# First layer of a two-block transformer kernel: value sums, merge and gate laid out by features, merging weights turned and repeated by DMA

## The reference, cut to what matters

```python
qkv = proj[..., :n_qkv].reshape(B, S, 3, N_DIL_GROUPS * DIL_HEADS, HEAD_DIM)
gate = proj[..., n_qkv:]
for g, (window, dil) in enumerate(DIL_GROUPS):       # (128,1), (512,4), (2048,16)
    o, lse = dilated_window_attention(q[:, :, sl], k[:, :, sl], v[:, :, sl], window, dil)
    outs.append(o); lses.append(lse)
alpha = jax.nn.softmax(jnp.stack(lses, axis=0), axis=0)
o = jnp.sum(alpha[..., None] * jnp.stack(outs, axis=0), axis=0)
y = o.reshape(B, S, DIL_WIDTH) * jax.nn.silu(gate)
return y @ w_out
```

## Time and profile before

| | |
|---|---|
| median of 3 runs | 2764.05 us (2762.17 to 2765.48) |
| profiled execution | 2763.36 us, span 2761.8 us |
| PE busy | 2699.4 us, 98% |
| PE weight loads | 2159.5 us, 78% |
| DVE, ACT, POOL busy | 1223.8, 1048.8, 1137.9 us |
| granted TensorE clock | 0.995 of full speed |
| chain that ended last | PE 93%, DVE 3%, ACT 2%, issue 1% |

### The profile page before, as it was taken

The page is one execution under the profiler, slowest core; times in us unless marked ns, Lnnn a source line. Parts: engine busy times, 40 slices in busy tenths (PEclk is TensorE's granted clock), DMA queues, the critical chain, the costliest instruction groups (busy, mean ns, idle before and its releaser), DMA issues.

```text
span 2761.8 us, 36052 instructions
## 1 busy us (share of the span) xinstructions
PE 2699.4 (98%) x13721; PEld 2159.5 (78%) x13721; DVE 1223.8 (44%) x2467; ACT 1048.8 (38%) x2005; POOL 1137.9 (41%) x894
## 2 busy tenths in 40 slices
PE   8999999999999999999999999999999999999998
PEld 6887878888778877776788888887777678888887
DVE  4434343443555356444236424265644423642425
ACT  3333434353345344452333424234445233342422
POOL 4434343434432443333364444444333336444442
PEclk9999999999999999999999999999999999999999
DMA  5434343432421332223252333324222325233331
GB/s 188 135 86 136 96 126 96 123 121 72 128 85 54 97 108 84 70 88 119 98 176 79 114 100 92 94 79 131 84 70 88 119 99 172 81 115 99 92 95 58
DMA packets 214912, 286.39 MB, mean 104 GB/s; under 512 B 16846, under 2 KB 154546, under 8 KB 213972
## 3 DMA queue, kind: packets, MB, share of 16 engines
q1 hardware_dynamic: 214740, 284.08, 33.6%
HBM read 248.31 MB, written 18.94 MB: 97 GB/s over the span
## 4 chain that ended last, share of the span: by engine, by line
PE 93%; DVE 3%; ACT 2%; issue 1%; POOL 0%; DMA 0%; DVEq 0%; ACTq 0%; POOLq 0%
PE banks L1652 37%; PE banks L1649 28%; PE banks L1645 13%; PE banks L1782 2%; PE banks L1670 2%; PE banks L1764 1%; PE banks L1868 1%; PE banks L1685 1%; PE banks L1709 1%; PE banks L1803 1%; PE banks L1891 1%; PE banks L1940 1%; PE banks L1854 1%; PE banks L1749 1%; PE banks L1825 1%
## 5 line engine op out<-in xcount | busy, mean ns | idle before, releaser
L2949 POOL TENSOR_TENSOR WS<-WR,WS 128x512 fp32r<-128x512 f32 (+2 forms) x676 | 854.2, 1295 | 1098.0 <-ACT WS L2003 1098.0
L1652 PE MATMUL banks<-WS,UT 128*128 128x512 f32 (+1 forms) x3696 | 800.3, 366 | 5.4 <-DVE UT L2360 5.4
L1652 PEld LDWEIGHTS banks<-WS,UT 128*128 128x128 f32 x3696 | 607.5, 190 | 135.7 <-issue 37.1
L1649 PE MATMUL banks<-UT,WS 128*128 128x512 f32 (+1 forms) x2832 | 661.3, 392 | 0.7 <-ACT AR L2190 0.7
L1649 PEld LDWEIGHTS banks<-UT,WS 128*128 128x128 f32 (+1 forms) x2832 | 526.7, 187 | 127.0 <-issue 17.0
L2003 ACT ACTIVATE WS<-WR 128x1024 fp32r<-128x1024 f32 (+1 forms) x344 | 333.0, 1018 | 223.0 <-PE banks L1652 153.6
L1645 PE MATMUL banks<-UT,WS 128*128 128x512 f32 x1536 | 374.1, 397 | 0.0
L1645 PEld LDWEIGHTS banks<-UT,WS 128*128 128x128 f32 x1536 | 283.4, 189 | 64.9 <-issue 6.2
L1652 PE MATMUL banks<-WS,AT 128*128 128x512 f32 x1296 | 308.2, 396 | 0.0
L2947 POOL TENSOR_TENSOR WS<-WR,WS 128x512 fp32r<-128x512 f32 x128 | 181.0, 1445 | 261.6 <-ACT WS L1999 261.6
L1652 PEld LDWEIGHTS banks<-WS,AT 128*128 128x128 f32 x1296 | 242.8, 188 | 58.2 <-ACT WS L2003 0.7
(11 more groups left out here) (225 smaller groups left out, 2679.2 us busy)
## 6 DMA issues: line engine op xcount, KB each, us to landing
WR<-in_w_in SPq DMA_DIRECT2D x112, 512.0 KB, 3.6
WR<-in_w_up SPq DMA_DIRECT2D x88, 512.0 KB, 3.5
WR<-in_dil_w_in SPq DMA_DIRECT2D x64, 512.0 KB, 3.9
WR<-in_w_down SPq DMA_DIRECT2D x40, 512.0 KB, 3.7
WR<-in_diff_w_in SPq DMA_DIRECT2D x32, 512.0 KB, 3.7
WR<-in_dil_w_in SPq DMA_DIRECT2D x32, 256.0 KB, 3.2
AR<-AF SPq DMA_DIRECT2D x128, 64.0 KB, 2.4
AR<-AF SPq DMA_DIRECT2D x64, 128.0 KB, 2.4
```

The lines of the kernel that those rows point to most:

```text
L1649: mm = pe.matmul(B[bank][0:c, :], w[part][:, kk, g * P:g * P + c], act[:, other, kk, :], start=start, stop=stop)
L1652: mm = pe.matmul(B[bank][:, off:off + n], act[:, other, before_k + kk, g * P:g * P + P], w[part][:, kk, :], start=start, stop=stop)
L2949: ge.tensor_tensor(slot(i, 1)[:, s], raw(i)[:, s], slot(i, 0)[:, s].bitcast(F32), ALU.subtract).then_inc(lo_p.sem, 1)
```

## The change

In `out1` the 64 columns of values are stationary and the turned weights move; head hh writes partitions 64·hh to 64·hh+63, and the order of the loops is key block outside, head inside. The sums so come out by features, far ones into `XT` (features x far order), near ones into `N0` (features x natural order), and only maxima and denominators (4 floats a token) go through `near`.

`merge1` is split. `share1` works out the shares on DVE; `rows1` turns the 128 x 16 shares into 16 rows by a PE transpose and an ACT eviction; `send1` stores the rows in DRAM (8 KB); `fetch1` loads them again, each row repeated over the 64 partitions of its head, by two DMAs of 256 KB; `merge1` then multiplies and adds by features. `send1`, `fetch1` and `merge1` are put into the list 2, 4 and 8 ticks after `rows1`.

The gate tiles become feature-major (`gates_by_features`), with `gate1` and `times1`, and the chunks with their 32 transposes are replaced by `parts1`, which makes high and low part from `XT` on ACT and DVE. R_G1 goes from 1.38 to 1.7.

```diff
-R0, R1, R2, R3, R_L1, R_L2, R_G1, R_G2 = 0.994, 1.0, 1.3, 0.54, 0.8, 1.2, 1.38, 1.35
+R0, R1, R2, R3, R_L1, R_L2, R_G1, R_G2 = 0.994, 1.0, 1.3, 0.54, 0.8, 1.2, 1.7, 1.35
+    def gates_by_features(self, ready, late):
+        for j in range(4):
+            while j < 3 and not ready(j):
+                self.tick()
+                yield 1
+
+            def deal(i, t, j=j):
+                self.step("gate1", i, t)
+                if j == 3:
+                    late.append((i, t, j))
+                else:
+                    self.step("times1", i, t, j)
+                    if j < 2:
+                        self.soon(4, lambda: self.step("parts1", 2 * j + t))
+            yield from self.feature_major(f"l1g{j}", deal)
...
                     self.step("weigh1", p)
                     yield
-                    self.step("merge1", p)
-                    merged.add(p)
+                    self.step("share1", p)
+                    yield
+                    self.step("rows1", p)
+
+                    def merge():
+                        self.step("merge1", p)
+                        merged.add(p)
+                    self.soon(2, lambda: self.step("send1", p))
+                    self.soon(4, lambda: self.step("fetch1", p))
+                    self.soon(8, merge)
                     yield
...
-        self.beside(self.gates("l1g", lambda j: 2 * j + 1 in merged, late), att, R_G1)
+        self.beside(self.gates_by_features(lambda j: 2 * j + 1 in merged, late), att, R_G1)
         self.lower(self.splits)
         self.drain(att)
+        self.flush()
...
-                       self.opening([("chunk", "l1g", c) for c in range(4, 8)]))
+                       self.opening([("parts1", c) for c in range(4, 8)]))
...
-                    for hh in range(2):
-                        r = 64 * hh
-                        for j in range(w // P):
+                    for j in range(w // P):
+                        for hh in range(2):
+                            r = 64 * hh
...
-                            mm = pe.matmul(B[ob][:, r:r + 64], fat(7168 + 512 * e + 256 * hh + j * P, P), vj,
+                            mm = pe.matmul(B[ob][r:r + 64, 0:P], vj, fat(7168 + 512 * e + 256 * hh + j * P, P),
                                            start=(j == 0), stop=(j == w // P - 1))
...
+                elif kind == "rows1":
+                    p, = a
+                    k = bank6["rows", p]
+                    pe.wait_ge(shared.sem, shared.at[p])
+                    pe.wait_ge(*before["rows", p])
+                    pe.transpose(B[k][0:16, 0:P], SM[:, QT + 16:QT + 32], IDN).then_inc(rows_turned.sem, 1)
...
+                elif kind == "merge1":
+                    p, = a
+                    by_rest = "p (l r) -> p r l"
+                    y, x = N0[p % 2].rearrange(by_rest, r=4), XT[:, p].rearrange("p (r l) -> p r l", r=4)
+                    s0, s1 = (shares[:, g].rearrange("p (r l) -> p r l", r=4) for g in range(2))
+                    ve.wait_ge(sums_out.sem, sums_out.at["1", l1_last(p, 1)])
+                    ve.wait_ge(rows_in, 32 * (p + 1))
+                    tt(y, y, s0, ALU.mult)
+                    tt(x, x, s1, ALU.mult).then_inc(dve_step, 1)
                     ve.wait_ge(dve_step, V.of())
+                    tt(x, x, y, ALU.add).then_inc(merged.sem, 1)
...
+                elif kind == "parts1":
+                    c, = a
+                    if c == 0:
+                        for name in "qk":
+                            se.wait_ge(*there(index[f"l1{name}23"]))
+                    if c == 4:
+                        se.wait_ge(merged.sem, merged.at[7])
+                    if c == 6:
+                        se.wait_ge(timed.sem, timed.at[index["l1g3"], 1])
+                    se.wait_ge(timed.sem, timed.at[index[f"l1g{c // 2}"], c % 2])
...
+                elif kind == "send1":
+                    p, = a
+                    sy.wait_ge(rows_out.sem, rows_out.at[p])
+                    if p > 0:
+                        sy.wait_ge(rows_sent, 16 * p)
+                    sy.dma_start(share_rows[p], turned_shares[0:16, :]).then_inc(rows_sent, 16)
+
+                elif kind == "fetch1":
+                    p, = a
+                    sy.wait_ge(rows_sent, 16 * (p + 1))
+                    if p > 0:
+                        sy.wait_ge(merged.sem, merged.at[p - 1])
+                    rows_of = share_rows[p].rearrange("(g r h) l -> h g r l", g=2, h=2)
+                    for h in range(2):
+                        sy.dma_start(shares[64 * h:64 * h + 64].rearrange("p g (r l) -> p g r l", r=4),
+                                     rows_of[h].unsqueeze(0).to_broadcast([64, 2, 4, P])).then_inc(rows_in, 16)
```

More of the change, by code:

```diff
@@ L991, in build @@
         pos_in = sem("pos_in")
+        rows_sent = sem("rows_sent")
+        rows_in = sem("rows_in")
         near_out = sem("near_out")
@@ L1083, in build @@
         merged = tally("merged")
+        shared = tally("shares")
         gated = tally("gated")
@@ L1252, in build @@
                 weigh_exp.plan(a[0])
+            elif kind == "share1":
+                shared.plan(a[0])
+            elif kind == "rows1":
+                k = takes_corner(("rows", *a))
+                rows_turned.plan(a[0])
+                freed[k] = rows_out.plan(a[0])
+            elif kind == "gate1":
+                i, t = a
+                tanhed.plan((i, t))
+                freed[order.bank[i, t][0]] = gated.plan((i, t))
+            elif kind == "times1":
+                timed.plan((a[0], a[1]))
+            elif kind == "parts1":
+                chunk_hi.plan(("l1g", a[0]))
+                chunk_lo.plan(("l1g", a[0]))
             elif kind == "merge1":
@@ L1484, in build @@
         H4, H0 = arr(4096, NB, D), arr(0, NB, D)
-        G0 = [arr(15360 + 528 * e, NB, 132) for e in range(2)]
-        Y0 = arr(16416, NB, 132)
+        XT = arr(0, KC, T)
+        N0 = [arr(15360 + 512 * e, T) for e in range(2)]
+        G0 = [arr(16384 + 16 * e, NB, 4) for e in range(2)]
+        Y0 = arr(16416, NB, 4)
+        turned_shares, shares = arr(16432, P), fat(2048, 2, T)
         M1, Z1 = ([view(SM[:, QT + 64 * e + 8 * i:QT + 64 * e + 8 * i + 8], (NB, 2)) for e in range(2)] for i in range(2))
@@ L2115, in scalar @@
                     se.activation(SM[:, QT + 16:QT + 32], SM[:, QT + 16:QT + 32], ACT.Exp).then_inc(weigh_exp.sem, 1)
+                elif kind == "rows1":
+                    p, = a
+                    se.wait_ge(rows_turned.sem, rows_turned.at[p])
+                    if p > 0:
+                        se.wait_ge(rows_sent, 16 * p)
+                    se.activation(turned_shares[0:16, :], B[bank6["rows", p]][0:16, 0:P],
+                                  ACT.Copy).then_inc(rows_out.sem, 1)
+                elif kind == "gate1":
+                    i, t = a
+                    se.wait_ge(proj.sem, proj.at[i, t])
+                    if (i - 1, t) in timed.at:
+                        se.wait_ge(timed.sem, timed.at[i - 1, t])
+                    se.activation(fat(3072 + 512 * t, 512), B[order.bank[i, t][0]][:, :], ACT.Tanh,
+                                  scale=0.5).then_inc(tanhed.sem, 1)
+                elif kind == "parts1":
+                    c, = a
+                    if c == 0:
+                        for name in "qk":
[5 more added lines that the diff above has]
+                    se.wait_ge(timed.sem, timed.at[index[f"l1g{c // 2}"], c % 2])
+                    se.activation(AT[:, 0, c, :].rearrange("p (l r) -> p r l", r=4),
+                                  XT[:, c, :].rearrange("p (r l) -> p r l", r=4), ACT.Copy).then_inc(chunk_hi.sem, 1)
                 elif kind == "gate":
@@ L2477, in vector @@
                     tt(d[:, 1], s, M1[p % 2], ALU.subtract).then_inc(weighed.sem, 1)
-                elif kind == "merge1":
+                elif kind == "share1":
                     p, = a
-                    z0, y = Y0[:, :, 130:132], Y0[:, :, 0:128]
+                    z0 = Y0[:, :, 2:4]
                     d, w, s = (view(SM[:, QT + o:QT + o + n], x) for o, n, x in
```

82 lines of the change are left out of this document (44 added, 38 removed).

## The result

The changed kernel takes 2794.09 us (median of 4 runs, 2792.39 to 2797.16); the kernel before took 2764.21 in its 4 runs (2762.17 to 2765.48). The ratio is 1.0107, 95% interval 1.0092 to 1.0122: slower by 30 us. Forecast were 2775 and at most 2786: the side was right, the size was not. The profiled run of after is its longest, 2797.16 us with a span of 2795.9, so its trace has some 3 us more than the median.

What follows compares the result with a forecast made beforehand. It took TensorE's in-order queue, busy 98% of the span, as the bound: 22.5 us of work saved against 33.9 of stands, net +11.4, so 2763.4 became 2774.8, or 2775 at the median's level; range 2752 to 2786.

Steps and rivals of the forecast that it cites:

- The stands of the row transposes: At the ends of head pairs TensorE waits at rows1 for share1 in DVE's queue: 21.6 us over eight places.
- The wait in front of the output projection: At layer one's tail TensorE stands 5.2 us before l1o2 for the DRAM round trip, merge and parts (bounds 0 and 10).
- shift and gate bursts: Next pair's units pushed one place, 2.0 us; attention steps in a row between feature-major gate steps, 5.1 us of waits.
- the price by L1891: out1's new form holds the queue 0.59 us per eight records, as in the second attention, against 0.855: 14.8 us saved.
- rival (d): In out1 the column halves run wholly side by side, eight records in 0.43 us: 9 us better, 2766; chance 0.04.
- 33.9 - 2.7 = 31.2: 33.9 us is the sum of TensorE's forecast stands; 2.7 is two idles between chunks and attention that go.
- TensorE work saved: Layer one: out1 14.8, gates 3.0, chunk transposes 3.0, idles 2.7, less added row transposes 1.0: 22.5 us.
- the idles: Two TensorE idles, 1.56 and 1.16 us, from bank turns between chunks and attention, go with the chunks: 2.7 us saved.
- the gates' form: Layer one's gate tiles as 48 matmuls of 512 columns instead of 96 of 256: 3.0 us saved (bounds 2 and 5).
- rival (e): Fetches landing in 8 to 10 us hold DVE at merge1 before score maxima, weight loads late: +22, 2786; chance 0.08.
- The last products: In layer one's tail before l1o2, DVE's second part was taken at 1.1 us, as such strided writes take 1.10.
- (b): share1 is ready at each of eight row transposes, so their 21.6 us vanish: 2753; chance 0.25 with milder mixtures below 2758.

Runs made afterwards that it cites:

- experiment four: The kernel before with only out1's matmuls changed to values stationary, so the sums reach the merge turned: 2757.3 us, ratio 0.9972.
- the fills: Two runs of the changed kernel with unread identity matmuls in front of the row transposes' waits: 130 of them 2795.22 us, 96 of them 2792.3.
- the later kernels: Changed kernel with share1 right behind weigh1, later row transposes, output blocks moved ahead, and merge1 of pairs 1, 3, 5 later still: 2760.85, 2760.62, 2760.35 us.
- the tuned form: Changed kernel with later row transposes, output blocks moved ahead, merge1 of pairs 1, 3, 5 at 11 or 20 ticks, or 11 with R_G1 1.38: 2760.85, 2760.62, 2760.35 us.
- second fill: The changed kernel with 96 unread identity matmuls in front of the row transposes' waits: 2792.3 us, ratio 1.0096.

## Why the prediction was wrong in size

**Right.** That TensorE's queue and not an engine's load decides, and where it would stand. The stands of the row transposes were forecast at 21.6 us, at pairs 0 to 6 as 2.4, 2.4, 1.7, 0, 2.4, 3.1, 4.0 and at pair 7 5.6; they measure 22.0: 2.23, 0, 2.23, 2.56, 1.46, 4.85, 3.73 and 4.94. It is pair 3 that stands, not pair 1, and pair 5's 4.85 against 3.1 is share1 lengthened beside POOL. The wait in front of the output projection is 6.6 for a forecast 5.2; those for exponents are 3.3 and, at out1, 1.3 more than before, under the 7.1 that shift and gate bursts were to cost. out1 itself saves 14.8 by starts of neighbours, what L1891 gave, and rival (d), halves wholly side by side, falls. Idle time in all rises by 34.7 us, for 33.9 - 2.7 = 31.2 forecast. That this is so close is in part luck: 5.0 us of waits for maxima, which the sum does not have, stand against some 2.5 too many for exponents.

**The step that failed.** "TensorE work saved: 14.8 + 3.0 + 3.0 + 2.7 - 1.0 = 22.5 us", set against the sum of stands, took all other matmuls to last as long as before. Without the idles, 19.8 of it is matmul time, and of that only 34.7 - 32.7 = 2.0 arrived. In the way of the other 17.8 stand, in the profiled run: clock loss on a TensorE at work, 12.1 against 1.7 (10.4); the matmuls in front of out1, 0.09 longer each as in experiment four (some 3.6); the turning transposes, which hold the queue for 28.2 in place of 25.5, since seven more of them have scores and no projection behind them (2.7); and the gates' form, which at the full clock saves 2.0 here (0.243 each, 46.7 in place of 48.7) and not 3.0 (1.0). So the largest missing term is the granted clock behind a stand, put at nothing; the second is the time that out1's new form adds in front of itself, which the price by L1891 left out though the trace of before has it. The changed kernel's profiled run is 3 us above its median. Over all its runs it has 27.2 us of clock loss against 15.2, 12 more, which at 0.7 is an estimate of some 8 us. What the experiments gave beyond idle time fits that: 2.6 to 6 from the fills, 5.8 and 4.7 where 8.1 and 18.5 us of idle time went.

**A wait that was missed.** With merge1 8 ticks late, the maxima of the next pair's near blocks stand behind it on DVE: TensorE waits 3.85 us at 371.59 and 1.14 at 518.69. The prediction's sum asked what was queued behind merge1 only at share1; rival (e) names the maxima, with slow fetches as the reason. Moving merge1 back behind the maxima shows the mechanism, on a kernel where it cost 8.1.

**The end of the layer.** The last products were priced by 1.10 us, a write that reads a bank. In the new form both operands are in SBUF. With POOL idle such a product takes 1.09 still (581.53), but the last three take 2.1 each beside a busy POOL:

```profile
581.53 1.09 DVE L2439 TENSOR_TENSOR AT<-AR,AT 128x512 fp32r<-128x512 f32 x1 [0.57 <-ACT AT L2193]
...
642.79 1.55 DVE L2439 TENSOR_TENSOR AT<-AR,AT 128x512 fp32r<-128x512 f32 x1 [1.94 <-ACT AT L2193]
645.60 6.25 DVE L2439 TENSOR_TENSOR AT<-AR,AT 128x512 fp32r<-128x512 f32 x3 [1.25 <-ACT AT L2193]
```

That is the likely reason why the later kernels keep 7 to 11 us there; it was read from rows and not tried by itself. The other part is that a chain of DMAs, merge and parts stands there with no projection left to lie beside it.

**Rivals.** (b) had the price of the eight waits right, 21.6 for the 23.2 that came back when they were taken out, but from a level that was 19 us too low: that run is at 2770.9 and not 2753. In the tuned form the change is a little faster than before, but only with the missed wait gone too. (e), slow fetches with maxima behind them, was given 0.08 and +22; its maxima are the 5.0 us, its share of the whole small. The granted clock as a multiplier of every stand was among no rival, and so the upper end, 2786, was too low.

## What to carry to other kernels

On a kernel whose TensorE is never idle, a new wait of TensorE costs more than its length: where the granted clock falls behind it, add for the matmuls that run at 1.2 GHz (here 5.8 us on 8.1, 4.7 on 18.5), and read the granted clock in windows of 5 us on both sides of each stand. When a DVE step that waits for a DMA is put into a list, write down everything that comes behind it on DVE until the data land, and who waits for that: here 3 ticks more for three of the eight merges were worth 13.9 us. When a small matmul group gets a new form, price it with the work on both sides: read how long the matmul in front of it holds the queue, too. Here 15.1 us less in out1, alone, shortened the kernel by 8.2, and 3.7 of the rest went into the matmuls in front.

## What the runs showed of the hardware

A granted clock that falls after so short a stand in an otherwise busy stretch was not expected: behind 2.80, 2.70 and 2.63 us (the row transposes put later, merge at 8 ticks) windows of 10 us read 0.66, 0.83 and 1.00. Nor is the length of one stand enough to tell: stands of 1.01 and 0.68 us close together (574.42 and 575.76, second fill) have a window at 0.83 around and behind them, and in the kernel before two of 0.69 (207.49 and 209.81) one at 0.83 behind them, while one of 2.56 (353.19, changed kernel) left it at 1.00. With TensorE kept busy over the waits of the row transposes the clock stayed up at each of these places.

Matmuls of 512 columns hold the queue for 0.237 us at the full clock, two of 256 columns for 0.253: over the gates 45.6 against 48.7 us for the same products.

A group with 64 stationary columns on column halves overlaps the matmul ahead of it by 0.09 us less than one with 128 (0.318 against 0.227 us for 512 columns). In front of the scores (64x128, 64x256) it is 0.318 as well.

DVE products with two operands in SBUF grow beside a busy POOL whatever their size: 128 x 8 from 0.17 to 1.23 us, 128 x 512 from 1.09 to 2.1; where one operand is a bank, 128 x 512 takes 1.10 beside a busy POOL too (616.25 in the kernel before). The Trainium skill, GPSIMD Engine Reference, "Specifications", names just this case, DVE instructions with two SBUF inputs, as in contention with POOL for the SBUF; the rows agree.
